# A GLA and stick-breaking decoder trunk: the lead goes from pairs to single blocks of 128 channels, and the gate bias moves into the stacked product

## The reference

```
cs = silu(c)
sh_a, sc_a, g_a, sh_m, sc_m, g_m = split(cs @ ada_w[0] + ada_b[0])
h = x * (1 + sc_a) + sh_a
q, k, v, r, gl = split(h @ w_in)            # 1024, 1024, 2048, 2048, 16 columns
log_a = log_sigmoid(gl @ w_gate_up + b_gate) / 16
bc = cumsum(log_a) within chunks of 64 tokens
q_dec, k_intra, k_state = q*exp(bc)/16, k*exp(-bc), k*exp(bc_last - bc)
```

## Time and profile before

| | us |
|---|---|
| median of 3 runs (2290.15 to 2291.61) | 2291.41 |
| the profiled execution's own time | 2290.08 |
| its span, first to last instruction | 2288.1 |
| PE busy / DVE busy / ACT busy | 2243.6 / 1719.3 / 1141.0 |
| lead on PE, first to last matmul | 25.4 to 146.3 |
| PE reaches `scores` (end of tile V+25) | 237.1 |

### The profile page before, as it was taken

The page is one execution under the profiler, slowest core; times in us unless marked ns, Lnnn a source line. Parts: engine busy times, 40 slices in busy tenths (PEclk is TensorE's granted clock), DMA queues, the critical chain, the costliest instruction groups (busy, mean ns, idle before and its releaser), DMA issues.

```text
span 2288.1 us, 31902 instructions
## 1 busy us (share of the span) xinstructions
PE 2243.6 (98%) x10980; PEld 1886.5 (82%) x10980; DVE 1719.3 (75%) x1678; ACT 1141.0 (50%) x1418; POOL 18.9 (1%) x42
## 2 busy tenths in 40 slices
PE   7999999999999999999999999999999999999998
PEld 5877778788888888888888888888888888888886
DVE  5669879888888888898876866887776545556656
ACT  2034355465555554444565555555555555444443
POOL 0000000000000000000000000000000000000000
PEclk9999999999999999999999999999999999999999
DMA  9987999859999999879858766883877555755563
GB/s 389 417 322 287 365 355 370 320 204 372 377 369 383 370 361 371 333 248 356 302 190 336 283 229 225 313 330 129 303 285 274 192 185 194 264 193 190 196 202 129
DMA packets 146474, 658.47 MB, mean 288 GB/s; under 512 B 16528, under 2 KB 16848, under 8 KB 115792
## 3 DMA queue, kind: packets, MB, share of 16 engines
q1 hardware_dynamic: 144000, 642.05, 75.8%
q0 software_dynamic: 2384, 15.24, 1.7%
HBM read 655.10 MB, written 2.13 MB: 287 GB/s over the span
## 4 chain that ended last, share of the span: by engine, by line
PE 87%; DVE 5%; DMA 5%; issue 2%; ACT 1%; SPq 1%; DVEq 0%; ACTq 0%
PE ps L1392 19%; PE ps L1294 17%; PE ps L1295 17%; PE ps L1298 17%; PE ps L1396 10%; PE ps L1308 2%; DMA R<-in_mods 2%; DVE mod_w L860 1%; DVE w_lo L855 1%; DMA S<-in_mods 1%; DMA mod_w<-in_mods 1%; DMA raw<-in_tiles 1%; PE ps L1426 1%; PE ps L1548 0%; PE ps L1494 0%
## 5 line engine op out<-in xcount | busy, mean ns | idle before, releaser
L855 DVE TENSOR_TENSOR w_lo<-raw,w_hi 128x1024 fp32r<-128x1024 f32 x720 | 877.5, 1224 | 462.7 <-ACT w_hi L427 456.9
L427 ACT ACTIVATE w_hi<-raw 128x1024 fp32r<-128x1024 f32 x720 | 760.6, 1059 | 829.2 <-PE ps L1298 380.3
L1294 PE MATMUL ps<-w_hi,h_both 128*128 128x512 f32 x1872 | 737.8, 394 | 2.7 <-ACT w_hi L427 2.7
L1295 PE MATMUL ps<-w_hi,h_both 128*128 128x512 f32 x1872 | 731.4, 391 | 0.0
L1298 PE MATMUL ps<-w_lo,h_both 128*128 128x512 f32 x1872 | 508.3, 391 | 8.0 <-DVE w_lo L855 7.7
L860 DVE SCALAR_TENSOR_TENSOR mod_w<-mod_w,cs 128x2048 f32<-128x2048 f32 x200 | 457.2, 2286 | 42.1 <-DMA mod_w<-in_mods 34.1
L1392 PE MATMUL ps<-h_both,w_hi 128*128 128x512 f32 x1920 | 480.9, 392 | 0.0
L1298 PEld LDWEIGHTS ps<-w_lo,h_both 128*128 128x128 f32 x1872 | 351.6, 188 | 85.7 <-DVE w_lo L855 12.4
L1294 PEld LDWEIGHTS ps<-w_hi,h_both 128*128 128x128 f32 x1872 | 352.7, 188 | 78.6 <-ACT w_hi L427 4.1
L1295 PEld LDWEIGHTS ps<-w_hi,h_both 128*128 128x128 f32 x1872 | 352.9, 188 | 72.7 <-issue 1.0
L1392 PEld LDWEIGHTS ps<-h_both,w_hi 128*128 128x128 f32 x1920 | 345.7, 189 | 61.6
(11 more groups left out here) (194 smaller groups left out, 1040.7 us busy)
## 6 DMA issues: line engine op xcount, KB each, us to landing
raw<-in_tiles SPq DMA_DIRECT2D x736, 512.0 KB, 4.8
mod_w<-in_mods SPq DMA_DIRECT2D x200, 1024.0 KB, 7.1
R<-in_mods SPq DMA_DIRECT2D x16, 1024.0 KB, 21.5
odd_raw<-in_tiles SPq DMA_DIRECT2D x16, 512.0 KB, 21.3
R<-in_tiles SPq DMA_DIRECT2D x16, 512.0 KB, 6.5
R<-in_ln_rows POOLq DMA_DIRECT2D x6, 1024.0 KB, 8.5
G<-in_mods SPq DMA_DIRECT2D x4, 1024.0 KB, 22.5
S<-in_mods SPq DMA_DIRECT2D x4, 1024.0 KB, 22.8
```

The source lines that it names most:

```text
L427: nc.scalar.activation(w_hi[:, slot, :], raw[:, slot, :], ACT.Copy).then_inc(hi_ready, 1)
L855: nc.vector.tensor_tensor(w_lo[:, slot, :], raw[:, slot, :], w_hi[:, slot, :].bitcast(F32), ALU.subtract)\
L1294: mm(dst, h_hi[:, kt, toks], w_hi[:, slot, c], start=start, stop=False, skip_group_check=more)
L1295: return mm(dst, h_lo[:, kt, toks], w_hi[:, slot, c], start=False, stop=False, skip_group_check=more)
```

## The change

- The lead runs by single blocks: SP queues two slabs (shift and scale of one block), two tiles, two slabs, two tiles; `lead_mod` works on two slabs, `coef` is made for one block, ACT releases each block by itself (`lead_h_full`), PE runs `lead_tile(kt, i)`, 16 groups of 32 instructions. The order of the slabs and of their biases in memory is changed to match.
- Slabs 32 and 33 are queued directly behind the lead, ahead of the first gv tiles. In gv the slabs are used behind V+0, V+1, V+2 (two), V+4, V+5, V+10 and V+15.
- The gate bias is no longer added by DVE. It is a row of `wgu` (in two parts, rows 96 and 97) against rows of ones in `gl_st`; `gates` multiplies 128 rows in place of 96. `gate_logits` and its sum are gone: `gate_log` and `log_sigmoid` read the product in `ps`. `bgt` and its load are gone; `wgu` has 128 rows in place of 96.
- The scan is cut in two halves, behind V+7 and V+8; `gate_rest` goes to V+2, `sums_to_end` to V+9, `gla_decayed` and the queries one tile later, `decays1` to `decays3` to V+9, V+11, V+12. ACT copies keys and queries out between its first four splits.
- The first gr body has 12 slabs in place of 10, the last go body 2 in place of 4 (behind positions 0 and 5).

```diff
-SCHEDULE = [("gv", 0, 1, 8), ("gv", 16, 1, 10), ("gr", 0, 1, 10), ("gr", 16, 1, 8), ("go", 0, 1, 8), ("go", 16, 1, 4), ("u0", 0, 1, 0), ("u0", 16, 7, 8),
+SCHEDULE = [("gv", 0, 1, 8), ("gv", 16, 1, 10), ("gr", 0, 1, 12), ("gr", 16, 1, 8), ("go", 0, 1, 8), ("go", 16, 1, 2), ("u0", 0, 1, 0), ("u0", 16, 7, 8),
...
-        GV_MODS = {0: (0,), 1: (1, 2), 2: (3, 4), 3: (5,), 14: (6,), 15: (7,)}
-        GV_MOD_LOADS = {3: (0, 1, 2), 4: (3,), 5: (4,), 6: (5,), 14: (6,), 15: (7,)}
+        GO_MODS = {0: (0,), 5: (1,)}
+        MODS_DONE = {T0["gv"]: {0: (0,), 1: (1,), 2: (2, 3), 4: (4,), 5: (5,), 10: (6,), 15: (7,)}, T0["go"] + 16: GO_MODS}
+        MODS_LOADED = {T0["gv"]: {3: (2, 3), 4: (4,), 5: (5,), 10: (6,), 15: (7,)}, T0["go"] + 16: GO_MODS}
...
             for pr in range(PAIRS):
-                for i in range(LEAD_MODS):
-                    load_lead(LEAD_MODS * pr + i)
...
-                for i in range(LEAD_TILES):
-                    t = LEAD_TILES * pr + i
-                    if pr >= 2:
-                        sp.wait_ge(tile_used, t - 2 * LEAD_TILES + 1)
-                    sp.dma_start(lead_raw(pr, i), tiles[t, :, :]).then_inc(lead_raw_loaded(pr, i), 16)
+                for k in range(2):
+                    for i in range(2):
+                        load_lead(LEAD_MODS * pr + 2 * k + i)
...
+                    for i in range(2):
+                        load_lead_tile(pr, 2 * k + i)
+            load_mod(LEAD, 0)
+            load_mod(LEAD + 1, 1)
...
             for pr in range(PAIRS):
-                act.wait_ge(lead_coef, pr + 1)
                 for kt in (2 * pr, 2 * pr + 1):
-                    ins = nc.scalar.activation(xT[:, kt, :], xT[:, kt, :], ACT.Identity, scale=coef[:, 0, kt:kt + 1], bias=coef[:, 1, kt:kt + 1])
-                ins.then_inc(h_full, 1)
+                    act.wait_ge(lead_coef, kt + 1)
+                    nc.scalar.activation(xT[:, kt, :], xT[:, kt, :], ACT.Identity, scale=coef[:, 0, kt:kt + 1], bias=coef[:, 1, kt:kt + 1])\
+                      .then_inc(lead_h_full, 1)
...
+            for i in range(TOK):
+                nc.scalar.activation(gl_st[6 * RANK:P, i * P:(i + 1) * P], ones[6 * RANK:P, :], ACT.Copy).then_inc(gl_copied, 1)
...
             def gate_log():
-                act.wait_ge(gate_sum, 1)
-                link(nc.scalar.activation(tmp_f, bc_f, ACT.Abs))
+                act.wait_ge(gate_done, 1)
+                link(nc.scalar.activation(tmp_f, logits_f, ACT.Abs))
...
-            for i in range(RING):
-                split_tile(V + i, i, lap_of(V) + 1, first=True)
-            for i in range(LEAD_TILES):
-                H[V + i].append(cols_out(i))
-            for at, f in ((3, gl_out), (4, gate_log), (5, gate_log2), (6, gate_log3), (8, decays1), (9, decays2), (10, decays3)):
+            for part in ((0, 1), (2,), (3,)):
+                for i in part:
+                    split_tile(V + i, i, lap_of(V) + 1, first=True)
+                for i in part:
+                    cols_out(i)()
+            for at, f in ((3, gl_out), (4, gate_log), (5, gate_log2), (6, gate_log3), (9, decays1), (11, decays2), (12, decays3)):
...
+                first, second = (ident[bias, 6 * RANK + i:6 * RANK + i + 1] for i in range(2))
+                link(nc.vector.tensor_tensor(coef2[bias, 0, 0:1], first, second, ALU.subtract))
+                link(nc.vector.tensor_scalar(wgu_hi[bias, :], wgu_hi[bias, :].bitcast(F32), coef2[bias, 0, 0:1], None, ALU.mult))
+                nc.vector.scalar_tensor_tensor(wgu_r[bias, :], wgu_f[bias, :], second, wgu_hi[bias, :].bitcast(F32), ALU.mult, ALU.add)\
+                  .then_inc(wgu_lo_ready, 1)
...
+            for kt in range(KT):
+                for i in range(2):
+                    lead_mod(2 * kt + i)
+                dve.wait_ge(mod_done, 2 * kt + 2)
...
+                if kt % 2 == 0 and kt:
+                    lead_h(kt // 2 - 1)
+                if kt == 2:
                     gl_split()
...
-            def gate_logits():
-                dve.wait_ge(gate_done, 1)
-                dve.wait_ge(setup_loaded, SETUP)
-                nc.vector.tensor_tensor(g3(bc_f), ps[:, 4:8, :].rearrange("p a (b t) -> p (a b) t", b=2),
-                                        bgt[:].unsqueeze(2).to_broadcast([P, GJ, SEQ]), ALU.add).then_inc(gate_sum, 1)
...
-            for at, f in ((1, gate_rest), (3, gate_logits), (6, log_sigmoid), (7, running_sums), (8, sums_to_end), (12, gla_keys(0)),
-                          (13, gla_keys(1)), (14, gla_decayed), (16, gla_queries(0)), (18, gla_queries(1)),
+            for at, f in ((2, gate_rest), (6, log_sigmoid), (7, running_sums(0)), (8, running_sums(1)), (9, sums_to_end), (12, gla_keys(0)),
+                          (13, gla_keys(1)), (15, gla_decayed), (17, gla_queries(0)), (19, gla_queries(1)),
...
-                    last = mm(ps[:, 4 + j // 2, (j % 2) * SEQ:(j % 2 + 1) * SEQ], wgu_r[0:6 * RANK, j * P:(j + 1) * P], gl_st[0:6 * RANK, :], start=True, stop=True)
+                    last = mm(ps[:, 4 + j // 2, (j % 2) * SEQ:(j % 2 + 1) * SEQ], wgu_r[:, j * P:(j + 1) * P], gl_st[:], start=True, stop=True)
```

More of the change, by code:

```diff
@@ L110, in lap_of, with build_kernel @@
     return (t - N_LEAD // 2 - early_before(t)) // RING
-def build_kernel(nc, tiles, mods, c_t, x_rows, mod_b, ln_t, b1_t, bg_t, w_gl, wgu, normg_t, ln_rows, b2_rows, out):
+def build_kernel(nc, tiles, mods, c_t, x_rows, mod_b, ln_t, b1_t, w_gl, wgu, normg_t, ln_rows, b2_rows, out):
     F32, F32R, BF16 = mybir.dt.float32, mybir.dt.float32r, mybir.dt.bfloat16
@@ L357, in _ @@
                                     pattern=[[-1, P]], channel_multiplier=1).then_inc(diag_made, 1)
-            for dst, src in ((lnt, ln_t), (b1t, b1_t), (bgt, bg_t), (normg, normg_t)):
+            for dst, src in ((lnt, ln_t), (b1t, b1_t), (normg, normg_t)):
                 pool.dma_start(dst[:], src).then_inc(setup_loaded, 16)
@@ L1300, in _, with lead_tile @@
             skipped = [N_LEAD]
-            def lead_tile(t, pr, i):
+            def lead_tile(kt, i):
+                pr, k = kt // 2, kt % 2
                 w = lead_raw(pr, i)
                 pe.wait_ge(lead_raw_loaded(pr, i), 16 * (pr // 2 + 1))
-                for k in range(2):
-                    kt = 2 * pr + k
-                    for blk in range(4):
-                        last = mm(ps[:, 2 * i + blk // 2, (blk % 2) * SEQ:(blk % 2 + 1) * SEQ], w[:, k * SW + blk * P:k * SW + (blk + 1) * P],
-                                  xT[:, kt, :], start=kt == 0 and blk % 2 == 0, stop=kt == KT - 1, skip_group_check=True)
-                last.then_inc(tile_used, 1)
+                for blk in range(4):
+                    last = mm(ps[:, 2 * i + blk // 2, (blk % 2) * SEQ:(blk % 2 + 1) * SEQ], w[:, k * SW + blk * P:k * SW + (blk + 1) * P],
+                              xT[:, kt, :], start=kt == 0 and blk % 2 == 0, stop=kt == KT - 1, skip_group_check=True)
+                if k == 1:
+                    last.then_inc(tile_used, 1)
             def stripe_tile(t, j, par, inputs=None):
@@ L1517, in _ @@
             pe.wait_ge(xt_copied, PAIRS)
-            for pr in range(PAIRS):
-                pe.wait_ge(h_full, pr + 1)
+            for kt in range(KT):
+                pe.wait_ge(lead_h_full, kt + 1)
                 for i in range(LEAD_TILES):
-                    lead_tile(LEAD_TILES * pr + i, pr, i)
+                    lead_tile(kt, i)
             def gate_inputs():
@@ L1753, in _layout @@
         "ln_t": np.concatenate([_cols(v[l, i]) for l, i in lns for v in (ln_g, ln_b)], axis=1),
-        "b1_t": np.concatenate([_cols(mlp_b1[l]) for l in range(2)], axis=1), "bg_t": _cols(gla_b_gate[0]),
+        "b1_t": np.concatenate([_cols(mlp_b1[l]) for l in range(2)], axis=1),
         "w_gl": w_in[:, 2 * qk + 2 * D:].reshape(KT, P, RANK).transpose(1, 0, 2),
-        "wgu": np.concatenate([gla_w_gate_up[0]] * 6), "normg_t": _cols(gla_norm_g[0]),
+        "wgu": np.concatenate([gla_w_gate_up[0]] * 6 + [gla_b_gate[0][None]] * 2 + [np.zeros((P - 6 * RANK - 2, qk), np.float32)]), "normg_t": _cols(gla_norm_g[0]),
         "ln_rows": np.stack([np.stack([_rows(v[l, i]) for v in (ln_g, ln_b)]) for l, i in lns]),
```

83 lines of the change are left out of this document (43 added, 40 removed).

## The result

The changed kernel takes 2278.21 us (median of 5 runs, 2275.99 to 2279.78) against 2291.41 before; the ratio is 0.9941, with a 95% interval from 0.9929 to 0.9953. It is faster by 0.6%. The forecast was 2279.4 in a range of 2271 to 2286. The profiled execution took 2278.66 us by itself (span 2276.9), 11.4 less than the one of before.

The account below looks back on a forecast made before the run. Loads were taken to bind the lead, and DVE's chain the stage up to `scores`. Gains of 9.2 us there and 1.5 in go made 10.7 off the profiled 2290.08: 2279.4, range 2271 to 2286 with rivals.

Parts of the forecast that it names:

- The first term: Up to the end of V+25, where `scores` starts: 9.2 us earlier, at 228 in place of 237.1.
- the second: Last go body: shorter waits for `w_lo` gain 1.5 us, between 0 and 2.4.
- The lead: Bound by loads; single blocks end it at 143.2, 3.1 us earlier, a gain gone again at `gates`.
- Ahead of `gates`: Slabs 34 and 35 hold up `gate_rest`; PE idles 3.1 us and `gates` starts at 157.2, 1.8 later than before.
- The gate chain: Behind `gates`: without `gate_logits`, `log_sigmoid` ends near 169.4, keys start at 186, 6 us earlier, and `scores` follows 42 later.
- The clock: PE's wait ahead of `gates` brings half clock and costs PE about 2.6 us, hidden behind DVE's chain.
- rival 2: Half clock delays ACT's splits and so DVE; keys late by 5.2 us, time 2284.6; chance 0.17.
- the third case below: Pointer from the clock step, for the lead's last pairs being slower; the listed third rival is "same", 2286.4, chance 0.10.
- The slots: 12 slabs in the first gr body cost 0, bound 2 us; fewer in the last go body gain 1.5.
- The first: Rival: DVE never late, PE's work bounds, `scores` at 219; 2269.7, or 2273 part of the way; chance 0.14.
- The third: Rival "same": loads pause 28 us at a share of 0.33 from 144 to 186, time 2286.4; chance 0.10.
- The fourth: Rival "slower": first gr body becomes bound by loads, taking 69 us at 304 GB/s; chance 0.04.

Follow-up runs that it names:

- pairs_back: The changed kernel with the lead in pairs again, in SP's queue and on PE: 2279.31 us, ratio 0.9944.
- x_first: The changed kernel with x and the gate weights queued behind the first slab in place of behind the second: 2279.04 us, ratio 0.9948.
- rest_first: The changed kernel with `gate_rest` behind V+1, ahead of slabs 34 and 35: 2277.22 us, ratio 0.9942.
- bias_back: The changed kernel with the gate bias added by DVE again (`gate_logits`, `bgt` load, 96 rows of `wgu`): 2281.42 us, ratio 0.9954.
- slabs_back: The changed kernel with gv's slab positions and loads as before and `gate_rest` behind V+1: 2281.04 us, ratio 0.9956.
- lead_and_slots: The changed kernel with the edits of slabs_back and bias_back both made: 2290.66 us, ratio 0.9997.
- slots_back: The changed kernel with 10 slabs in the first gr body and 4 in the last go body, as before: 2281.66 us, ratio 0.9956.
- gv_8_slabs: The changed kernel with two slabs moved from the second gv body to the second gr body: 2282.00 us, ratio 0.9959.
- the two with half tiles: The changed kernel and gv_8_slabs, each with the tiles of gr and go loaded by half: 2276.57 and 2274.29 us.

## Why the prediction was right

**The sum.** It had 9.2 us up to `scores` and 1.5 behind it; the trace has 9.58 and 1.54. The time is 2278.66 for the profiled execution where the sum gave 2279.4. The first term came out by its mechanism, with errors that partly cancel; the second by luck, as shown under the slots.

**The lead.** Right that it would end near 143.2 (142.65), right that the loads bind it, and right that the gain would be gone at `gates`; pairs_back shows that. The time at which the first slab pair lets block 0 start was wrong: x stands behind both slabs now and lands at 16.3 us, so PE starts at 26.04, not earlier than the 25.4 of before. x_first shows that this is worth nothing.

**Ahead of `gates`.** I had slab 34 done at 152.4, slab 35 at 156.7 and `gates` at 157.2 behind 3.1 us of idle PE. They are done at 151.2 and 154.9, and `gates` starts at 155.47 behind 2.22 us. The mis-sized term is the load of slab 35, 5.9 us in my sum after the earlier trace rows and 5.24 in the trace, and slab 32 was done 0.7 us earlier than I had it (144.0, not 144.7). I had named a start of `gates` well before 156 as a sign of being wrong; 155.47 is near that line, and rest_first shows how little hangs on it: 2.2 us there are 0.65 at the keys.

**The gate chain.** `log_sigmoid` ends at 168.75 (forecast 169.4), the keys start at 184.53 (186), and from there to `scores` it takes 43.0 us (42), so that errors of 1.5 and 1.0 us partly cancel. The reason that I gave for the gain, a `gate_logits` that is gone, was one of two, and they work together. With the slabs moved the bias on DVE costs 3.2 us (bias_back; 0.4 of it the add in the chain, 1.3 the lead), with the add gone the slabs cost 2.8 (slabs_back), and both together 12.4 (lead_and_slots): before, each made the other dear.

**The clock.** The step that failed. I wrote that the wait ahead of `gates` should be followed by half clock, for 2.6 us. The wait was 2.22 us, and the window from 145 to 180 has 1.00. Since that loss was counted as hidden, the sum did not move, and rival 2, which rested on it, did not come about. The Trainium skill ("TensorE: Matmul & The Clock Gate", section "HAM oscillation — how this bites in real kernels") describes waits that are longer than the pieces of matmul work between them. The lead's waits, 0.9 to 1.0 us ahead of some of its runs, are far shorter than the matmuls between them (10.63 us behind the last one), so that section did not speak against the single blocks, as my prediction had it; in this trace the lead runs at 0.97 as before. The prediction also calls this the third case below, but its third rival is about loads.

**The slots.** I priced the 12 slabs in gr at nothing with a bound of 2, and the relief in go at 1.5. The first gr bodies show no wait, as said, though the share is 0.97 from 250 to 278. What I did not see is how near the loads are to the limit up to 410 us: two more slabs in gr and 3.8 us are lost. In the last go body I expected no wait over 0.5 us, and one of 1.01 us is left at 423.16; a new one of 0.59 stands at 403.61. The slots were worth 2.3 us by the stretch and 3.4 by the medians (slots_back), not 1.5. Against it stands some loss in the stretch, which takes 216.23 us with the slabs back and 218.44 without. That an early `scores` leaves the loads less time would explain this, but it is not shown: the difference is within the scatter of the stretch, and lead_and_slots has the latest `scores` and still takes 219.18. My sum had no such loss in it; that the trace has 1.54 where I wrote 1.5 is luck.

**The rivals.** The first, PE's own work as the bound, fails at `scores`, which would have come at 219. The third, pausing loads, asked for a share of 0.33 from 144 to 186 us; it was 0.81 from 145 to 180. The fourth, loads that bind gr, did not come about with 12 slabs, since PE does not wait in gr; with two more slabs it does (gv_8_slabs), and it costs 3.8 us where I had priced 15.

## What to carry to other kernels

Before an operation is taken out of a chain, look at what stands ahead of it in its engine's order: here an add of 2.3 us and slabs that waited for their loads cost 12.4 us together, and about 3 each when the other was mended, because the add kept ACT's passes from running beside the slabs. Read the order of the queue and the order of the engine together, and undo parts in pairs as well as singly, since the single edits showed only half of the joint price. And when work is moved into a later stage, look at the loads there first: two slabs moved behind `scores` lost 3.8 us with the DMA share at 0.98, and gained 2.3 with half the bytes per tile.

## What the hardware showed that was not expected

Waits of PE of nearly one length were followed by different clocks. Ahead of `gates`, 2.22 us (changed), 2.29 (x_first and bias_back), 2.45 and 2.47 us (the two with half tiles) were followed by full clock: eight matmuls in 1.21 or 1.22 us. The same matmuls took 2.07 us behind 2.37 us (slots_back) and 2.35 us (gv_8_slabs), and the window from 145 to 160 has 0.89 there. The longer waits, 2.90 with 0.61 in the kernel before, 3.19 (slabs_back) and 3.59 (lead_and_slots), were all followed by half clock. Further on, the waits near 405 us of 2.15 (pairs_back) and 2.42 us (x_first) were followed by a mean clock of 0.61 over 4.4 us and 0.70 over 5.7 us. So the length of the wait alone does not decide between 2.15 and 2.5 us; what does is open.
